# A second norm that sums in PSUM with a place per tile, and copies and stores that change engines

## The reference, cut to what matters

```python
z = x @ w_in                            # q, k, v of 3 head groups | conv x_in, B, C | gate_a, gate_c
A = dilated sliding-window attention    # windows 128, 512, 2048, dilations 1, 4, 16, rotary q and k
Cv = B * conv3(C * x_in)
mix = (sigmoid(gate_a) * (A @ W_pa) + sigmoid(gate_c) * (Cv @ W_pc)) @ W_out
h = LN1(alpha * x + mix)                # alpha = 2 ** 0.25
y = LN2(alpha * h + PEER(h))            # PEER: 8 heads, product keys over 128 x 128 experts, top 16
```

## Time and profile before

| what | value |
|---|---|
| median of three runs | 4798.47 us |
| the profiled execution, its own time | 4800.55 us |
| its span, first to last instruction | 4799.0 us |
| granted TensorE clock, mean | 0.889 of full speed |
| TensorE matmul busy | 3962.5 us |
| VectorE busy | 3043.2 us |
| ScalarE busy | 1179.5 us |
| GpSimd busy | 1759.1 us |
| moved by DMA | 982.63 MB, 205 GB/s in the mean |

### The profile page before, as it was taken

One profiled execution on the slowest core, in us unless ns is written; L12 is line 12 of the kernel. 1 busy time (PEld: TensorE's weight loads), 2 busy tenths in 40 slices (PEclk: granted clock), 3 DMA queues, 4 the chain that ended last, 5 costly groups with the idle time before them and its releaser, 6 DMA issues. The chain is left out here.

```text
span 4799.0 us, 64513 instructions
## 1 busy us (share of the span) xinstructions
PE 3962.5 (83%) x24889; PEld 3686.0 (77%) x24889; DVE 3043.2 (63%) x5862; ACT 1179.5 (25%) x2121; POOL 1759.1 (37%) x1228
## 2 busy tenths in 40 slices
PE   7897979798999897798066489888888888888882
PEld 7796969657999896687055488888888888888882
DVE  3332323212222234399888699989998999999984
ACT  1212121311111101143289122222222222222221
POOL 0000000000000002377500566666766666666644
PEclk8787879899999999888589699999999999999996
DMA  5433332252111244110024899999999999999973
GB/s 154 152 99 122 108 113 65 78 218 73 59 60 60 85 130 141 56 31 10 0 124 193 333 359 357 355 350 362 360 355 358 348 359 359 356 356 354 358 271 112
DMA packets 470701, 982.63 MB, mean 205 GB/s; under 512 B 49022, under 2 KB 267518, under 8 KB 467427
## 3 DMA queue, kind: packets, MB, share of 16 engines
q0 software_dynamic: 156704, 619.52, 34.6%
q1 hardware_dynamic: 312578, 355.11, 21.8%
q10 hardware_dynamic: 1152, 4.46, 0.2%
HBM read 901.43 MB, written 131.28 MB: 215 GB/s over the span
## 5 line engine op out<-in xcount | busy, mean ns | idle before, releaser
L1879 POOL DMA_INDIRECT u_row<-in_peer_u_dram,eid x512 | 785.1, 1533 | 703.1 <-DVE dots L1938 417.7
L59 PE MATMUL e_ps<-coef_h,v_h 128*128 128x288 f32 x2048 | 661.3, 323 | 243.6 <-DVE v_l L1907 199.4
L59 PE MATMUL e_ps<-hBh,u_h 128*128 128x288 f32 x2048 | 607.4, 297 | 62.8 <-DVE u_l L1900 62.8
L1954 DVE SCALAR_TENSOR_TENSOR f_row<-v_row,g_coef,f_row 128x1024 f32<-128x1024 f32 x508 | 650.9, 1281 | 6.1 <-DMA v_row<-in_peer_v_dram,eid 5.6
L1885 POOL DMA_INDIRECT v_row<-in_peer_v_dram,eid x512 | 573.1, 1119 | 197.4 <-issue 154.2
L59 PEld LDWEIGHTS e_ps<-coef_h,v_h 128*128 128x128 f32 x2048 | 414.8, 203 | 298.1 <-DVE v_l L1907 244.9
L60 PE MATMUL e_ps<-coef_l,v_h 128*128 128x288 f32 x2048 | 634.4, 310 | 0.0
L61 PE MATMUL e_ps<-coef_h,v_l 128*128 128x288 f32 x2048 | 632.1, 309 | 0.0
L1938 DVE CUSTOM_DVE_ANT_0 u_row<-u_row,h_row 128x1024 f32<-128x1024 f32 x512 | 620.9, 1214 | 10.1 <-DMA u_row<-in_peer_u_dram,eid 10.0
L61 PE MATMUL e_ps<-hBh,u_l 128*128 128x288 f32 x2048 | 607.0, 296 | 0.0
L60 PE MATMUL e_ps<-hBl,u_h 128*128 128x288 f32 x2048 | 606.9, 296 | 0.0
(11 more groups left out here) (282 smaller groups left out, 8469.9 us busy)
## 6 DMA issues: line engine op xcount, KB each, us to landing
u_raw<-in_peer_uT_dram SPq DMA_DIRECT2D x128, 512.0 KB, 9.0
v_raw<-in_peer_vQ_dram SPq DMA_DIRECT2D x256, 256.0 KB, 8.5
s_g<-gate_block SPq DMA_DIRECT2D x9, 4096.0 KB, 11.2
x_gate<-s_g SPq DMA_DIRECT2D x64, 576.0 KB
out_o_kv_sample_dram<-in_cache_kv_w_dram POOLq DMA_DIRECT2D x2, 16256.0 KB, 94.6
c_raw<-in_w_in_dram SPq DMA_DIRECT2D x40, 512.0 KB, 3.8
w_raw<-in_w_in_dram SPq DMA_DIRECT2D x96, 192.0 KB, 3.7
cache_v<-in_cache_vS_dram SPq DMA_DIRECT2D x8, 2304.0 KB
```

The lines of the kernel that those rows point to most:

```text
L59: pe.matmul(out, lh, rh, start=first, stop=False)
L1879: pool.indirect_dma_start(urow[:, r % RING], None, io["peer_u"][0], bass.IndirectOffsetOnAxis(ap=eid[:, r:r + 1], axis=0)).then_inc(urow_i ...
L1954: dve.scalar_tensor_tensor(out=f, in0=vrow[:, r % RING], scalar=coef[:, s % 2, x:x + 1], in1=f, op0=ALU.mult, op1=ALU.add).then_inc(weighe ...
```

## The change

Three things change.

1. The cache copies leave `prompt_attn`. All four are now issued by GpSimd at the start of `conv_gates`, one behind the other, without a wait ahead of them.
2. The gate stores in `conv_gates` are issued by ScalarE, behind each group of three sigmoids and a wait for the last of them. GpSimd only waits for the stores and frees the buffer.
3. `ln2_out` is written anew. The tiles of `acc` (4 to 8) come first. Every tile has its own place for h, and the row tiles one for f, so SyncE issues all loads at once and waits for nothing. TensorE forms alpha * h + f in PSUM: one matmul with alpha times the identity against h, and one with the identity against f, or eight with blocks of `acc` against the identity. There are four places in PSUM. VectorE takes the statistics from PSUM and makes the whole affine step in two instructions, of which the second writes over h. GpSimd is idle. ScalarE takes the roots and issues the stores, and waits for them once at the end.

```diff
@@ prompt_attn, gpsimd
             for s in range(SP):
-                pool.wait_ge(w_lo_done, s * 6 + 6)
-                for g, a, b in ((0, 0, 120), (1, 0, 504)) if s == 0 else ((2, (s - 1) * 508, s * 508),) if s < 3 else ():
-                    pool.dma_start(io[f"o_kv{g}_sample"][0, :, a:b].rearrange("b r w s2 e -> b (r w s2 e)"),
-                                   io[("cache_kv_w128", "cache_kv_w512", "cache_kv_w2048")[g]][0, :, DS + a:DS + b]
-                                   .rearrange("b r w s2 e -> b (r w s2 e)")).then_inc(k["cache_moved"], 16)
                 pool.wait_ge(at_done, 2 * (s + 1))
                 pool.dma_start(io["s_att"][s][:, :SEQ], attS[:]).then_inc(att_out, 16)
@@ conv_gates, gpsimd
             pool.sem_inc(gate_free, 2)
+            for g, a, b in ((0, 0, 120), (1, 0, 504), (2, 0, 508), (2, 508, 1016)):
+                pool.dma_start(io[f"o_kv{g}_sample"][0, :, a:b].rearrange("b r w s2 e -> b (r w s2 e)"),
+                               io[("cache_kv_w128", "cache_kv_w512", "cache_kv_w2048")[g]][0, :, DS + a:DS + b]
+                               .rearrange("b r w s2 e -> b (r w s2 e)")).then_inc(k["cache_moved"], 16)
             with pool.Fori(0, KD) as j:
-                for x in range(2):
-                    pool.wait_ge(z_act, j * AJ + ((2 + x) * NC + AJ))
-                    pool.dma_start(io["s_gate"][x][j], gate[:, x]).then_inc(gate_out[x], 16)
                 for x in range(2):
                     pool.wait_ge(gate_out[x], (j + 1) * 16)
                     pool.sem_inc(gate_free, 1)
@@ conv_gates, scalar
+                    if m >= 3:
+                        act.wait_ge(z_act, q * (2 * AJ) + (i // NU * AJ + (m - 1) * NC + AJ))
+                        act.dma_start(io["s_gate"][m - 3][bass.ds(q * 2 + i // NU, 1)].rearrange("o p n -> (o p) n"),
+                                      gate[:, m - 3]).then_inc(gate_out[m - 3], 16)
@@ ln2_out, rewritten (its core)
+    ORDER = tuple(range(GTILES, NT)) + tuple(range(GTILES))
+    NY = 4
...
+            for i, t in enumerate(ORDER):                      # sync
+                n = rows_of(t)
+                sp.dma_start(H[:n, t], io["s_h"][t * P:t * P + n]).then_inc(h_in[t], 16)
                 if t < GTILES:
+                    sp.dma_start(F[:, t], io["s_f"][t * P:(t + 1) * P]).then_inc(h_in[t], 16)
+                if i == 0:
+                    sp.dma_start(gain[:], io["ln2_g"].to_broadcast([P, D])).then_inc(consts, 16)
+                    sp.dma_start(bias[:], io["ln2_b"].to_broadcast([P, D])).then_inc(consts, 16)
...
+                if i >= NY:                                    # tensor, tile i of ORDER
+                    pe.wait_ge(centred, i - NY + 1)
+                pe.wait_ge(h_in[t], 32 if t < GTILES else 16)
+                for a in range(2):
+                    cols = slice(a * 512, (a + 1) * 512)
+                    pe.matmul(ps[:n, i % NY, cols], scaled_id[:n, :n], H[:n, t, cols], start=True, stop=False)
+                    if t < GTILES:
+                        m = pe.matmul(ps[:n, i % NY, cols], k["ident"][:], F[:, t, cols], start=False, stop=True)
+                    else:
+                        for j in range(4 * a, 4 * a + 4):
+                            m = pe.matmul(ps[:n, i % NY, j * P:(j + 1) * P], k["acc"][:, j, t * P - TA:t * P - TA + n],
+                                          k["ident"][:], start=False, stop=(j % 4 == 3))
...
+            def stats(i):                                      # vector
+                n, x = rows_of(ORDER[i]), i % 2
+                dve.wait_ge(y_ready, i + 1)
+                for a in range(2):
+                    dve.bn_stats(st[:n, x, 6 * a:6 * a + 6], ps[:n, i % NY, 512 * a:512 * (a + 1)])
+                dve.drain()
+                dve.bn_aggr(mv[:n, x], st[:n, x]).then_inc(var_ready, 1)
+
+            def finish(i):
+                t, x = ORDER[i], i % 2
+                n = rows_of(t)
+                dve.wait_ge(std_ready, i + 1)
+                dve.reciprocal(rstd[:n, x:x + 1], std[:n, x:x + 1])
+                dve.scalar_tensor_tensor(out=H[:n, t], in0=ps[:n, i % NY], scalar=mv[:n, x, 0:1], in1=gain[:n],
+                                         op0=ALU.subtract, op1=ALU.mult).then_inc(centred, 1)
+                dve.drain()
+                dve.scalar_tensor_tensor(out=H[:n, t], in0=H[:n, t], scalar=rstd[:n, x:x + 1], in1=bias[:n],
+                                         op0=ALU.mult, op1=ALU.add).then_inc(done, 1)
+
+            stats(0)
+            dve.wait_ge(consts, 32)
+            for i in range(NT):
+                if i + 1 < NT:
+                    stats(i + 1)
+                finish(i)
...
+            root(0)                                            # scalar
+            for i in range(NT):
+                if i + 1 < NT:
+                    root(i + 1)
+                store(i)
+            act.wait_ge(y_out, 16 * NT)
```

More of the change, by code:

```diff
@@ L2043, in ln2_out, with sb @@
 def ln2_out(nc, io, k):
+    ORDER = tuple(range(GTILES, NT)) + tuple(range(GTILES))
+    NY = 4
     with ExitStack() as c:
+        def sb(n, s):
+            return c.enter_context(nc.sbuf_tensor(n, s, F32))
         def sem(n):
             return nc.alloc_semaphore(n)
[L2048 to L2056, removed]
+        H, F = sb("f_h", [P, NT, D]), sb("f_rows", [P, GTILES, D])
+        gain, bias, eps = sb("n2_gain", [P, D]), sb("n2_bias", [P, D]), sb("n2_eps", [P, 1])
+        scaled_id = sb("f_alpha", [P, P])
+        st, mv = sb("n2_st", [P, 2, 12]), sb("n2_mv", [P, 2, 2])
+        std, rstd = sb("n2_std", [P, 2]), sb("n2_rstd", [P, 2])
+        ps = c.enter_context(nc.psum_tensor("f_ps", [P, NY, D], F32))
+        h_in = [sem(f"f_h_in{t}") for t in range(NT)]
+        consts, alpha_ready = sem("n2_consts"), sem("f_alpha_ready")
+        y_ready, var_ready, std_ready = sem("f_y_ready"), sem("n2_var_ready"), sem("n2_std_ready")
+        centred, done, y_out = sem("n2_centred"), sem("n2_done"), sem("y_out")
         block = c.enter_context(nc.Block())
@@ L2060, in _ @@
         def _(sp):
[L2061 to L2064, removed]
-                sp.dma_start(N.res[:n, x], io["s_h"][t * P:t * P + n]).then_inc(h_in[x], 16)
-                if t < GTILES:
-                    sp.dma_start(frow[:n, x], io["s_f"][t * P:t * P + n]).then_inc(h_in[x], 16)
-        def loaded(t):
-            return sum(2 if u < GTILES else 1 for u in range(t % 2, t + 1, 2))
+            for i, t in enumerate(ORDER):
+                n = rows_of(t)
+                sp.dma_start(H[:n, t], io["s_h"][t * P:t * P + n]).then_inc(h_in[t], 16)
+                if t < GTILES:
+                    sp.dma_start(F[:, t], io["s_f"][t * P:(t + 1) * P]).then_inc(h_in[t], 16)
+                if i == 0:
+                    sp.dma_start(gain[:], io["ln2_g"].to_broadcast([P, D])).then_inc(consts, 16)
+                    sp.dma_start(bias[:], io["ln2_b"].to_broadcast([P, D])).then_inc(consts, 16)
@@ new lines, in _ @@
+        @block.tensor
+        def _(pe):
+            pe.wait_ge(alpha_ready, 1)
+            for i, t in enumerate(ORDER):
+                n = rows_of(t)
[11 more added lines that the diff above has]
+                                          k["ident"][:], start=False, stop=(j % 4 == 3))
+                m.then_inc(y_ready, 1)
@@ L2113, in _, with root @@
-        @block.tensor
-        def _(pe):
-            for t in range(GTILES, NT):
-                x, n = t % 2, rows_of(t)
-                pe.wait_ge(staged, t - GTILES + 1)
-                pe.wait_ge(N.summed, t + 1)
-                for j in range(KD):
-                    m = pe.transpose(ps[:n, x, j * P:(j + 1) * P], stage[:, x, j, :n], k["ident"][:])
-                m.then_inc(f_ready, 1)
+            def root(i):
+                n, x = rows_of(ORDER[i]), i % 2
+                act.wait_ge(var_ready, i + 1)
+                act.activation(std[:n, x:x + 1], mv[:n, x, 1:2], ACT.Sqrt, bias=eps[:n]).then_inc(std_ready, 1)
@@ L2124, in program, with store @@
+            def store(i):
+                t = ORDER[i]
+                dst = io["o_y_prompt"][0, t * P:(t + 1) * P] if t < PT else io["o_y_sample"].rearrange("b s d -> (b s) d")
+                act.wait_ge(done, i + 1)
+                act.dma_start(dst, H[:rows_of(t), t]).then_inc(y_out, 16)
+            root(0)
[4 more added lines that the diff above has]
+            act.wait_ge(y_out, 16 * NT)
 def program(nc, io, phases=99):
```

37 lines of the change are left out of this document (5 added, 32 removed).

## The result

| | before | after |
|---|---|---|
| median | 4814.88 us (4 runs, 4792.62 to 4831.89) | 4957.30 us (4 runs, 4905.89 to 4960.44) |
| profiled span, mean granted clock | 4799.0 us, 0.889 | 4958.4 us, 0.875 |

The ratio after to before is 1.0288, with a 95% interval of 1.0218 to 1.0359. The change costs about 142 us by the medians. The direction and the main mechanism were as forecast; 4957.3 us lies 2.3 us above the upper end of the range, 4955. The forecast set out from a median of 4798.47 us of the kernel before; with one run more that median is 4814.88, so as a change the result is +142 us where +112 was forecast.

What follows compares the result with a forecast made beforehand. TensorE and its clock were taken to bound the attention and convolution stage, and a GpSimd-and-store loop the norm. 4800.5 - 57 + 205 + 2 - 38 = 4912.5 us profiled, giving 4910 us; range 4828 to 4955.

Steps and rivals of the forecast that it cites:

- the main mechanism: Convolution stage: the first weight load lands only when the cache copies end, so TensorE stands; +205 us.
- One for one: DMA queues: GpSimd's copy queue and SyncE's load queue pass equal packet counts, 166 each in 50 us, 64.5 KB against 0.5 KB.
- The rival by which loads pass between the copies: Convolution stage: several small pieces served per large one; near 4710 us if freely (chance 0.05), near 4800 if partly (0.08).
- +205 us: Convolution stage: copies take 208 us, so the first weight load lands near 1355 us instead of 1150.4.
- The light half: Convolution stage: the half of the DMA engines given 20.6 MB of copies, expected done after 143 us.
- the 59 to 73 that I had: Convolution stage: us the half of the engines with 33.2 MB needs for its last 12.6 MB, alone.
- lets 64 small ones through: one single load: Convolution stage: 64 large packets on each of 8 engines let 64 small ones pass, one 512 KB weight load.
- -57 us: Attention, copies taken out: 66.6 us of stalls gone, less about 12 us of remaining pauses, plus 2 us for round 0's clock.
- in all three rounds: Attention, rounds 0 to 2: the clock falls at the remaining 4 us pause behind unit 8; part of -57 us.
- the bounds are -55 and -148: Attention, copies taken out: the limits set around the -57 us term.
- The gate stores, +2: Convolution stage, stores issued by ScalarE: three stand at a loop boundary, 3 * 0.6 = +2 us; bounds 0 and 16.
- The norm, -38: Second norm rewritten: VectorE bounds at 4.4 us a tile, ending at 4760.7 instead of 4799; -38 us.

Runs made afterwards that it cites:

- the fill at the entry: Nine thrown-away matmuls a round at the attention units' entry, added to the changed kernel without cache copies: 4688.97 us, 0.9758 of the kernel before.

## Why the prediction was right, and where its sizes were off

**One for one was the number that mattered, and it held:** 64.5 KB against 512 bytes with two copies (191 to 191) and with one (87 to 87), and 4 KB against 512 bytes (2918 to 2917). The rival by which loads pass between the copies, with its turns of nine or more pieces, did not occur at any piece size. The typical 9 to 17 descriptors per turn of the Trainium skill, "DMA: Bandwidth & Descriptors", section "Queues, rings and completion order", are not what these traces' packets show; a packet in the trace is one piece.

**+205 us came out as +215, by two errors against each other.** The copies took 240.7 us, not 208. I had added the rates of the halves, 2 * 144 = 288 GB/s; both together moved 12.37 MB in 50 us, 247 GB/s. The light half was through some 170 us behind the first issue instead of 143, and the heavy half took 72 more, at the top of the 59 to 73 that I had. Against that, two units' loads got through, some 29 us of work, while I had none landing before the end. The step "lets 64 small ones through: one single load" left out the packets of 4 bytes, 896 in the stage, of which 272 lie in one stretch of 15 us.

**-57 us came out as -13: here the clock was placed wrongly.** The stalls went as forecast, from 66.6 to 1.9 us, and the long issue is gone. Two parts of the term did not hold.

- *Rounds 0 to 2 gave 45 us, not 57.* The forecast let the clock fall in the 4 us behind unit 8, "in all three rounds", which makes 122 us for a round on average. After the change it fell at the entry to the units in each of them, and a round took 126. Rounds 1 and 2 of before had entered at full clock. That the fall behind unit 8 is the cheaper one is shown by the round 1 without copies and by the fill at the entry: 117.8 and 118.3 us.
- *Round 3 took 36 us back.* The prediction named "the bounds are -55 and -148", with round 3's 88.6 us as the floor to which the others could come down, and took round 3 as fixed. In the profiled execution it went up to 124.8 us. The new code in the attention did not do it: the same attention had 88.6 us in the run with the copies alone and 126.4 in the one with the copies in the retrieval, and the run at 4905.89 us of the kernel after lies 51 us below the others, somewhat more than one round's clock.

So the entry is a place where the clock may hold or fall in every round, and a term with both signs. The upper bound should have been about -57 + 12 + 36 = -9 us, and the range would have reached some 5000. Why it holds at one entry and falls at another, and how often in the kernel after, stays open; four runs can't say it.

**The gate stores, +2:** three boundaries at 1.0 us, +3.

**The norm, -38:** -40.8 in the profile, -34 by the medians of the run with the norm alone. The first h took 4.17 us and not 3.5, a pass from PSUM 1264 ns and not 1221, but the period is 4.07 us and not 4.4: from the last pass of one tile to the aggregate of the next the chain has 1.28 us for both statistics and the drain behind them, where the forecast had 1.37 and the drains on top, and the reciprocal does not stand in it. VectorE bounds, as forecast, and GpSimd is idle.

**What the change was worth.** By the medians, taking the copies out of the attention gives some 54 us (31 by the profiled spans), putting them in the convolution stage costs 234, the norm gives 34. The copies at a quiet place with the drain out of their way, and TensorE kept busy at both places where its clock falls, give a kernel at 0.9652 of the time of before with all its outputs.

## What to carry to other kernels

Before a large DRAM-to-DRAM copy is moved, look up what else uses the queues at the new place, in packets and not in bytes: with one packet for one, a 512-byte load beside 64 KB pieces is served at 1/126 of the copy's rate, and pieces of 4 KB take most of that back. Then look what the issuing engine does next: a drain on GpSimd behind its own DMAs stood until they had landed. And where a stage swings in time by a fixed amount from run to run, look for a place where TensorE's clock may hold or fall; a few matmuls that nobody reads can settle it, and were worth more here than everything the change set out to win.

## What the runs showed of the hardware that was not expected

- GpSimd's drain stood 181.65 us, until the copies that GpSimd had issued were through; with a semaphore in its place there was no pause.
- Packets of 4 bytes count as full turns for the other queue: in 15 us 272 of them let as many 512-byte pieces through.
- Two copies on both halves of the engines moved 247 GB/s together, one alone on its half 189 GB/s (5.66 MB in 30 us; before, 10.71 MB in 50 us).
- SyncE can be held inside a single issue while a copy runs in GpSimd's queue: 66.62 us before, with pieces of 64 KB, and up to 18.6 us with pieces of 4 KB, where eight loads of 192 KB went out in 54.92 us instead of 4.34. In the convolution stage, with two loads under way at most, each issue took 0.37 to 0.43 us.
- In the stretches read, the granted clock after a fall at the units' entry stays at 0.50 for the rest of the round; after a fall behind unit 8 it came back once, within 7 us.
- With 9 and 28 further matmuls a round (at the entry, and between units 2 and 11) it stayed at 1.00 throughout, for 24 to 32 us a round.
